# Late modulation chunks in context tile 0, a fixed alternation of expert groups, and output products ahead of the values

## The reference

```python
sh_a, sc_a, gt_a, sh_f, sc_f, gt_f = adaln_params(c, w_mod[l], b_mod[l])
hl = modulate(xl, g_attn[l], sh_a, sc_a)
out_lat, out_ctx = token_mixers(hl, hc, l, not last, w_in[l], ...)
xl = xl + gt_a * out_lat
hl = modulate(xl, g_ffn[l], sh_f, sc_f)
xl = xl + gt_f * expert_choice_ffn(hl, w_router[l], w_gate[l], w_up[l], w_down[l])

def expert_choice_ffn(h, w_router, w_gate, w_up, w_down):
    gates, idx = lax.top_k(affinity, cap)      # cap: 64 latent, 32 context tokens per expert
    a, u = xs @ w_gate, xs @ w_up              # xs: the tokens that each expert chose
    y = (silu(a) * u) @ w_down * gates
```

## Time and profile before

| | us |
|---|---|
| median of three runs | 2147.86 |
| lowest, highest | 2144.3, 2151.32 |
| profiled execution | 2151.53 |
| its span | 2149.7 |
| TensorE busy in the span | 1969.2 (92%) |
| VectorE, ScalarE, GpSimd busy | 664.1, 529.6, 156.6 |
| DMA | 515.66 MB, mean 240 GB/s |
| TensorE's mean granted clock | 0.975 |

### The profile page before, as it was taken

The page is one execution under the profiler, slowest core; times in us unless marked ns, Lnnn a source line. Parts: engine busy times, 40 slices in busy tenths (PEclk is TensorE's granted clock), DMA queues, the critical chain, the costliest instruction groups (busy, mean ns, idle before and its releaser), DMA issues. The chain is left out here.

```text
span 2149.7 us, 27244 instructions
## 1 busy us (share of the span) xinstructions
PE 1969.2 (92%) x10872; PEld 931.5 (43%) x10872; DVE 664.1 (31%) x1746; ACT 529.6 (25%) x1222; POOL 156.6 (7%) x155
## 2 busy tenths in 40 slices
PE   5999989999979999999999899889997998888875
PEld 2436465556642332323323556455554333333322
DVE  3322345666540100101001632366665011110203
ACT  3211154665531000100100421165554110000001
POOL 1101010000010010020100101100001000000000
PEclk9999979999989999999999999999998999999998
DMA  9742020000089999999999402020017899999995
GB/s 353 291 159 81 0 79 1 1 2 1 36 332 414 423 364 418 378 390 421 364 414 421 150 20 79 17 82 1 21 40 286 352 427 426 426 427 427 427 427 217
DMA packets 90935, 515.66 MB, mean 240 GB/s; under 512 B 10594, under 2 KB 15628, under 8 KB 36540
## 3 DMA queue, kind: packets, MB, share of 16 engines
q1 hardware_dynamic: 84496, 493.29, 56.8%
q0 software_dynamic: 4416, 15.21, 2.4%
q10 hardware_dynamic: 1900, 5.43, 0.6%
HBM read 498.69 MB, written 15.20 MB: 239 GB/s over the span
## 5 line engine op out<-in xcount | busy, mean ns | idle before, releaser
L739 PE MATMUL psS<-arena 128*64 128x512 f32 (+9 forms) x4552 | 1158.5, 556 | 71.1 <-DMA arena<-in_w_up 22.0
L739 PEld LDWEIGHTS psS<-arena 128*64 128x64 f32 (+4 forms) x4552 | 456.1, 159 | 666.9 <-issue 585.9
L1961 DVE TENSOR_REDUCE mx<-psS 128x1 f32<-128x768 f32 (+2 forms) x200 | 165.5, 827 | 153.0 <-PE psS L739 151.3
L1307 ACT ACTIVATE arena<-psT 128x768 f32<-128x768 f32 (+7 forms) x261 | 150.1, 577 | 245.7 <-PE psT L742 232.0
L742 PE MATMUL psT<-ident,arena 128*128 128x128 f32 (+1 forms) x1036 | 172.7, 290 | 36.1 <-ACT arena L1307 9.1
L1307 ACT ACTIVATE arena<-psS 128x128 f32<-128x128 f32 (+5 forms) x158 | 61.8, 421 | 571.6 <-PE psS L739 525.7
L2145 DVE TENSOR_TENSOR arena<-arena,psS 128x512 f32<-128x512 f32 x32 | 20.6, 684 | 549.2 <-PE psS L739 549.2
L742 PEld LDWEIGHTS psT<-ident,arena 128*128 128x128 f32 (+1 forms) x1036 | 120.1, 145 | 135.5 <-issue 97.8
L739 PE MATMUL psT<-arena 128*32 128x512 f32 x1536 | 174.5, 595 | 0.0
L1307 ACT ACTIVATE arena<-psS,nb 128x768 f32<-128x768 f32 (+2 forms) x200 | 157.9, 792 | 1.4
L739 PE MATMUL psM<-arena 128*128 128x512 f32 x288 | 140.9, 611 | 0.0
(11 more groups left out here) (226 smaller groups left out, 1266.5 us busy)
## 6 DMA issues: line engine op xcount, KB each, us to landing
arena<-in_w_gate SPq DMA_DIRECT2D x117, 1024.0 KB, 21.3
arena<-in_w_up SPq DMA_DIRECT2D x116, 1024.0 KB, 22.5
arena<-in_w_down SPq DMA_DIRECT2D x116, 1024.0 KB, 25.9
arena<-in_w_mod SPq DMA_DIRECT2D x48, 1024.0 KB, 7.2
arena<-in_w_in SPq DMA_DIRECT2D x6, 2048.0 KB, 7.8
arena<-in_w_out SPq DMA_DIRECT2D x8, 512.0 KB, 7.8
arena<-in_w_out SPq DMA_DIRECT2D x2, 2048.0 KB, 15.4
normed_rows<-arena ACTq DMA_DIRECT2D x8, 512.0 KB, 7.3
```

The costliest lines, as they stand in the source:

```text
L739: return nc.tensor.matmul(o, lhsT, rhs, start=start, stop=stop)
L1307: return nc.scalar.activation(o, i, f, **kw)
L1961: link(V.reduce_max(mx[:, par:par + 1], view(S, 0, P, 0, (512, 2), (1, n)), axis=AX.XY))
```

## The change

The chunks of both late groups are loaded into four places of 1 MB in the region of the output weights (`late_slot`): two once the fourth section is done, the others once the projections are finished, each waiting for the chunk four before. TensorE multiplies them in steps 0 to 11 of context tile 0 (`LATE_AT`), into bank 7 for the first group and bank 5 for the second; ScalarE copies the rows at steps 6 and 12, TensorE turns the groups at steps 16 and 24 (`LATE_TURN_AT`), VectorE copies the columns. The router biases move from steps 3 and 5 to 7 and 8, the gates from 7, 9, 11, 13 to 9, 11, 13, 15. The output weights are loaded behind the chunks, in six transfers. The rings carry expert weights alone. `AHEAD_OF_GATHER` is gone; in the second layer slot 15 waits for the gathered rows.

In the first layer's expert loop every stage has an order of its own: 0, 1, 2 or 2, 0, 1 by `STAGE_ORDER`. Hidden rows are turned in the order 2, 0, 1, and tokens in pairs at four places. Counts and waits follow the orders.

In every attention step of both layers the bias, the gate and the output pieces are issued ahead of the values.

```diff
-AHEAD_OF_GATHER = 6
-GATE_AT = ((7, 9, 11, 13), (9, 11))
-BIAS_AT = ((3, 5), (7,))
+GATE_AT = ((9, 11, 13, 15), (9, 11))
+BIAS_AT = ((7, 8), (7,))
-MOD_LATE, MOD_LAST = KD, KD
-LAST_MOD_AT = {"turn": 13, "columns": 14}
+LATE_AT = {0: (0, 1), 1: (2, 3), 2: (4,), 3: (5,), 4: (6,), 5: (7,), 7: (8, 9), 8: (10, 11), 9: (12,), 10: (13,), 11: (14, 15)}
+LATE_ROW_AT = {6: 0, 12: 1}
+LATE_TURN_AT = {TURNS: 0, TURNS + 8: 1}
+LATE_BANK, LATE_TURN_BANK = (7, 5), 5
+LATE_SLOTS = 4
-TURN_AT = {(8, 1): (0,), (8, 2): (1,), (9, 0): (2,), (9, 1): (3,), (9, 2): (4,), (10, 0): (5,), (10, 1): (6,), (10, 2): (7,)}
+CLL, LLC = (2, 0, 1), (0, 1, 2)
+HIDDEN_AT = {(7, 0): 2, (7, 1): 0, (8, 2): 1}
+STAGE_ORDER = (LLC, CLL, LLC, CLL, LLC, CLL, LLC, CLL, CLL, LLC, CLL, LLC)
+TURN_AT = {(8, 1): (0, 1), (9, 1): (2, 3), (10, 2): (4, 5), (11, 1): (6, 7)}
...
+        def late_slot(c):
+            return WOUT + (4096, 6144, 0, 2048)[c % LATE_SLOTS]
+        def order(l, q, st):
+            if l:
+                return (0, 1)
+            return (2, 0, 1) if q * NSTAGE + st == NQ * NSTAGE - 1 else STAGE_ORDER[st % NSTAGE]
...
+                def late_chunk(c):
+                    _, r, k = MOD_CHUNKS[MOD_FRONT * KD + c]
+                    if c >= LATE_SLOTS:
+                        sp.wait_ge(s_mused, MOD_FRONT * KD + c - LATE_SLOTS + 1)
+                    load(ar[:, late_slot(c):late_slot(c) + SLOT], A["w_mod"][L - 1, k * P:(k + 1) * P, r * 2048:(r + 1) * 2048], s_w[c % 8])
...
+                if l == 0:
+                    sp.wait_ge(z["proj"], NSTEP - TT)
+                    for c in range(2):
+                        late_chunk(c)
                 sp.wait_ge(z["proj"], NSTEP)
...
+                    for c in range(2, 2 * KD):
+                        late_chunk(c)
+                for n, k in enumerate((4, 6, 0, 2)):
+                    if l == 0:
+                        sp.wait_ge(s_mused, (MOD_FRONT + 2) * KD - LATE_SLOTS + n + 1)
...
                     if l and j == NSLOT[l] - 2:
                         sp.wait_ge(z["fgev"], 4 * L)
+                        sp.wait_ge(s_g[1], 16 * L)
-                    if l == 0 and j == FIRST[l] + AHEAD_OF_GATHER:
-                        sp.wait_ge(s_g[2], 16)
...
                         last.then_inc(z["T"], 1)
+                    for c in LATE_AT.get(s, ()) if l == 0 else ():
+                        if c == KD:
+                            pe.wait_ge(z["me"], turns_through(PLANS[l], ("Q", 1, "B1")))
+                        late_mod(c)
+                    if l == 0 and s in LATE_TURN_AT:
+                        g = LATE_TURN_AT[s]
+                        pe.wait_ge(z["me"], turns_through(PLANS[l], ("Q", 2, "B1") if g else ("Q", 1, "C1")))
+                        mod_transpose(MOD_FRONT + g, LATE_TURN_BANK)
+                    if s in BIAS_AT[l]:
+                        router_bias(BIAS_AT[l].index(s))
+                    if s in GATE_AT[l]:
...
+                        gates(2, "gt", (7, 7, 7, 7), (n,))
+                    for x in pieces:
+                        output_piece(*x)
                     if pv is not None:
...
-                    for x in pieces:
-                        output_piece(*x)
                     for x in turns:
...
-                late = range(MOD_FRONT * KD, (MOD_FRONT + 1) * KD) if l == 0 else ()
-                for n in late[:6]:
-                    late_mod(n)
...
-                            for m in last_late[:4]:
-                                late_mod(m)
...
-                    for m in last_late[4:] if l == 0 else ():
-                        late_mod(m)
...
-                        for g in last_order(l) if (q, st) == (NQ - 1, NSTAGE - 1) else range(NX):
-                            if st == 8 and g == 1 and wc:
-                                turn_hidden(q, 2)
+                        for g in (last_order(l) if not wc and (q, st) == (NQ - 1, NSTAGE - 1) else order(l, q, st)):
                             group(q, st, g)
-                            if st == 7 and g == 1:
+                            if wc and (st, g) in HIDDEN_AT:
+                                turn_hidden(q, HIDDEN_AT[st, g])
...
+                    if l == 0 and s in LATE_ROW_AT:
+                        modulation_row(LATE_ROW_AT[s])
...
-                    for g in range(NX):
+                    for g in hidden_order(l):
                         act.wait_ge(z["done"], groups_done(l, q, 3, g))
```

More of the change, by code:

```diff
@@ L430, in backbone_program, with stage_done @@
         s_w = [sem(f"ring_slot{i}") for i in range(max(NSLOT))]
-        MOD_FILLS = [MOD_FRONT if i < KD else 0 for i in range(max(NSLOT))]
+        MOD_FILLS = [L * 3 if i < KD else 0 for i in range(max(NSLOT))]
         NLOAD = NQ * NSTAGE * QUAD
-        FIRST, LAST = (MOD_LATE, 0), (MOD_LAST, 0)
         def slot_filled(l, j):
-            j += FIRST[l]
             i = j % NSLOT[l]
-            earlier = MOD_FILLS[i] + sum(i < NSLOT[k] and (FIRST[k] + NLOAD + LAST[k] - 1 - i) // NSLOT[k] + 1 for k in range(l))
+            earlier = MOD_FILLS[i] + sum(i < NSLOT[k] and (NLOAD - 1 - i) // NSLOT[k] + 1 for k in range(l))
             return s_w[i], 16 * (earlier + j // NSLOT[l] + 1)
-        def late_bank(g):
-            return 7 if g == MOD_FRONT else 3
+        def late_slot(c):
[4 more added lines that the diff above has]
+            return (2, 0, 1) if q * NSTAGE + st == NQ * NSTAGE - 1 else STAGE_ORDER[st % NSTAGE]
         def groups_done(l, q, st, g):
-            return l * NQ * NSTAGE * (SW[0] // P) + (q * NSTAGE + st) * (SW[l] // P) + g + 1
+            return l * NQ * NSTAGE * (SW[0] // P) + (q * NSTAGE + st) * (SW[l] // P) + order(l, q, st).index(g) + 1
+        def stage_done(l, q, st):
+            return groups_done(l, q, st, order(l, q, st)[-1])
         def halves_through(l, i, r):
@@ L979, in _ @@
                         scores(0)
-                    if l and tau == 3:
-                        pe.wait_ge(s_mrow, 3 * L)
-                    if l and tau == LAST_MOD_AT["turn"]:
-                        mod_transpose(MOD_FRONT + 1, 5)
                     for i in k_jobs(tau - 1):
@@ L1210, in turn_hidden @@
                         last.then_inc(z["hp"], 1)
-                        free[6 + b] = (z["he"], 2 * hidden_tile(l, q, g) - 1 + b)
-                last_late = range((MOD_FRONT + 1) * KD, len(MOD_CHUNKS))
+                        free[6 + b] = (z["he"], 2 * hidden_turn(l, q, g) - 1 + b)
                 def combine(q):
@@ L1248, in group @@
                         pe.wait_ge(z["ge"], KD * (q + 1) - 4)
-                    elif q == 0 and m == 0 and g == 0:
+                    elif q == 0 and m == 0 and g == order(l, q, st)[0]:
                         pe.wait_ge(z["ge"], kq + 1)
@@ L1261, in group @@
                         experts, n, col = range(QUAD), CAP_C, 256
-                        for e in experts if (q, st) == (NQ - 1, NSTAGE - 1) else ():
+                        for e in experts if order(l, q, st)[0] == g else ():
                             pe.wait_ge(*slot_filled(l, (q * NSTAGE + st) * QUAD + e))
@@ L1778, in _ @@
                         mod_columns(MOD_T_AT[tau])
-                    if l and tau == LAST_MOD_AT["columns"]:
-                        mod_columns(MOD_FRONT + 1, 5)
                     if tau < NSTEP and uses_dve(*STEPS[tau]):
@@ L2005, in _ @@
                         router_weights()
+                    if l == 0 and s in LATE_TURN_AT:
+                        mod_columns(MOD_FRONT + LATE_TURN_AT[s], LATE_TURN_BANK)
                     for x in summed:
```

123 lines of the change are left out of this document (54 added, 69 removed).

## The result

The changed kernel takes 2166.44 us (median of 4 runs, 2162.38 to 2168.87) against 2148.79 for the kernel before on the same chip: ratio 1.0079, 95% interval 1.0060 to 1.0098. The forecast was 2135.7 with a range of 2126 to 2149; sign and size were wrong. Medians and intervals here are of fast runs; one slow execution of e2 (3338 us) is left out of its interval. The profiled execution of the changed kernel has a span of 2166.8 us, 17.1 above that of before (2149.7).

What follows compares the result with a forecast made beforehand. TensorE was taken to pace the first expert loop with DMA close behind, the weight stream the second. Terms +7 - 2.3 - 3.1 - 3.7 - 0.7 - 5.3 - 0.7 - 3.4 = -12.2 us gave a median of 2135.7, range 2126 to 2149.

Steps and rivals of the forecast that it cites:

- Weights waits: First expert loop: TensorE's waits for weights fall from 4.4 to 1 us, gain 3.4 us (0 to 4.4).
- the rival to which I gave 0.17: First expert loop: weights become the bound and eat the order's and waits' gains, no change, 2145.1 us; chance 0.17.
- My own sign of being wrong: Wrong would be, among others, waits on weights of more than 5 us in the first expert loop.
- Alternation and turns: First expert loop: fewer changes of shape between groups gain 5.3 us, paired token turns 0.7 us.
- Tile 0: Context tile 0, first layer's attention: the moved modulation chunks cost +7 us (3.6 to 17).
- About 22 us: Tile 0, steps 7 to 11: chunks, bias blocks, gates and own work take about 22 us, putting step 12 at 310.
- steps 0 to 5 follow the chunks (to 288): Tile 0: the first six steps are paced by the chunks' arrival, until 288 us.
- Idle time takes in part of the chunks: Tile 0: TensorE's idle 8.8 us, including 1.45 before step 1 and 1.84 ahead of turned outputs, absorbs some chunk work.
- The rival that the clock stays low: Tile 0: TensorE runs at 1.2 GHz between chunk waits; whole tile low gives 2156.7 us, slower; chance 0.10.
- First gather: First layer, ahead of the expert loop: the gather no longer queues behind weights, gain 3.1 us (0 to 3.1).
- second, -3.7 and -0.7 for the projections: Second layer: earlier gather gains 3.7 us (0 to 3.7); a modulation turn leaving the projections gains 0.7 (0 to 1.5).
- End of the first loop: Chunks leave the combine products: first latent product 1.0 us earlier, VectorE's normalised rows then limit; gain 2.3 us together.

Runs made afterwards that it cites:

- e2: Kernel before with only the new expert order (alternating stages, paired token turns, context hidden tile first): 2152.1 us, ratio 1.0023.
- e14: e13 with the new expert order on top: 2137.6 us, ratio 0.9957 to the kernel before.
- e13: Kernel before; gathers for quads 3 and 4 after stage 5, sums' store and load at stage 9, second layer's slot 15 waits for gathers: 2140.2 us, 0.9968.
- e16: Changed kernel, all chunk products but only chunks 0 to 3 loaded, same edit as e6 run again: 2161.7 us, ratio 1.0069.
- e6: Changed kernel with all chunk products, but only chunks 0 to 3 loaded and no wait for the others: 2159.7 us, ratio 1.0042.
- e7: Kernel before with three instead of six weights ahead of the first gather, and second layer's slot 15 waiting for the gathers: ratio 1.0009.
- e4: Changed kernel with the values back ahead of late chunks, router bias, gates and output products in each attention step: ratio 1.0077.

## Why the prediction was wrong, step by step

**Weights waits, forecast -3.4, measured +12.** The step that failed reads "should fall to 1, as 16.8 MB leave a stream of nearly the same length as TensorE's work". The 16.8 MB left at the loop's two ends; the waits stand at stages 3 to 7 of each quad, and nothing had left there. I had divided a total by a total where the trace had five waits, all on in_w_up and so in stages 4 to 7. The next sentence, that a context-first stage needs its last two weights 3.5 us earlier, named the mechanism and priced it at the 1 us left. It was worth about 2.5 us in each quad and 1 more at stage 3 of quads 2 to 4, and it was the rival to which I gave 0.17; and that rival, as I had sized it, stopped at eating the gain. My own sign of being wrong, over 5 us of such waits, came. The DMA share of 0.99 was no measure of slack either: e14's loop is 10 us shorter at a share of 1.00, with 406 GB/s instead of 401.

**Alternation and turns, forecast -6.0, measured -7.5 of TensorE's time** (e13 to e14). Right, a little small. In the changed kernel it is: +12.3 of waits (16.4 of weights and 0.3 for ScalarE, against 4.4), +3.1 for two groups at half clock, -7.5, which makes +7.9 against 8.3 read.

**Tile 0, forecast +7, measured +14.7** (+13.7 between the means of seven profiles each). "About 22 us" for steps 7 to 11 measured 22.15 (296.58 to 318.73), by luck: what I counted there adds up to some 18.6 us (eight chunks at 0.89, bias blocks of 3.43 in all, two gates at 1.02, five times 1.2), and 1.6 of the 22.15 are two chunks at half clock. The failing step is the one before it, "steps 0 to 5 follow the chunks (to 288)": I added the 22 us to 288, as if step 7 began there. Step 6 and the own work of the steps ahead of it were missing, and the low clock from 283 to 290 us lies in them too; step 7 began at 296.58. "Idle time takes in part of the chunks" failed too. Of the idle 8.8 us, 1.45 stand ahead of the first scores and 3.3 behind step 12; 3.7 are left where the chunks went, and there the changed kernel still idles 4.7 (1.09, 3.18 and 0.43). The stall ahead of the turned outputs stayed at 2.16 us where I let it take 1.5 back. The products had to be paid for the most part: 10.6 us of 14.3 even with the clock nearly full (0.96, e16).

**The clock in tile 0.** The rival that the clock stays low did not decide. In 272 to 319 us it was 0.89 after and 0.77 before, and 0.96 in e16. Dips still make the spread between executions (e6 is 5.7 us over e16). Two windows of the changed kernel:

```profile
280.00:285.00 5.00, 1.82 (x10) 0.20 (x9) 0.79 (x4) 1.10 (x4) 0.00 (x0) 0.81 0.96 356
285.00:290.00 5.00, 5.00 (x24) 2.25 (x20) 0.88 (x3) 1.02 (x4) 0.00 (x0) 0.51 1.01 426
```

The dip stands behind the 3.18 us wait, and in 290 to 300 us the clock is at 1.00 again. The later one, at 303.36, has TensorE busy throughout and no wait ahead of it. The Trainium skill, TensorE: Matmul & The Clock Gate, section "HAM oscillation — how this bites in real kernels", says that bursts with DMA waits between them can run at half rate one after another; the trace shows one such stretch here, of some 7 us from 283 to 290 in steps 2 to 4, and not all of steps 1 to 5. The 0.50 in 275 to 280 us of the kernel before, which I counted for the rule, doesn't bear on it: the waits ahead of it were for ScalarE (1.14 and 0.39 us), not for DMA.

**First gather, forecast -3.1, measured -2.4; second, -3.7 and -0.7 for the projections, measured -3.7 together.** The waits in both layers are about what the prediction named (4 us), 3.5 and 4.8 us:

```profile
651.00 1.13 PE L772 MATMUL psS<-ident,arena 128*128 128x128 f32 x4 [3.54 <-DMA arena<-normed_rows,LIU]
...
1687.83 1.13 PE L772 MATMUL psS<-ident,arena 128*128 128x128 f32 x4 [4.83 <-DMA arena<-normed_rows,LIU]
```

e7 adds that in the first layer the gain hangs on a full ring: with three weights held back the gather came 2.2 us sooner and the loop gave back 7.

**End of the first loop, forecast -2.3, measured +1.2** (-0.9 to +1.2 in the experiments with the same tail). The first latent combine product did come 1.0 us nearer, 5.84 us behind the first context product (1207.03) instead of 6.86. But where four chunks had kept TensorE busy it now waits, and goes on at 1.2 GHz:

```profile
1212.87 0.79 PE L769 MATMUL psS<-output_high,selection 128*128 128x512 f32 x1 [3.73 <-DVE output_low L2184]
1213.46 0.63 PE L769 MATMUL psS<-output_low,selection 128*128 128x512 f32 x1
```

Twelve products there start 0.43 us apart and not 0.23: 2.4 us. Behind them TensorE waits 2.27 us for VectorE's rows, as foreseen, and its first eight transposes take 1.97 us instead of the 1.09 of before, at half clock again. I had counted the chunks as work removed and not as what held the clock up.

**Order ahead of the values, forecast 0:** right (e4). **Second expert loop unchanged:** right, 474.98 against 474.85.

## To carry to other kernels

Slack of a stream against an engine is a matter of places, not of totals: list the waits with their times, find what other transfer stands ahead of each, and ask how many buffers are in hand there. An order that needs a buffer sooner spends that slack, and the place of side transfers can be worth more than the order itself: with the new order it was worth 16.2 us of loop (548.8 in e2, 532.6 in e14), the order with the transfers moved 4.3 (e13 to e14). Work that sits where TensorE would otherwise wait, such as the chunks between the combine products, costs little, and here the clock stayed up behind it (1.00, against 0.50 without); moved to where idle time exists only on average, it was paid for the most part.

## What I had not expected of the hardware

Behind a wait of 2.5 us TensorE's next group sometimes took 5.1 to 5.3 us (half clock for part of it) and sometimes 3.64: waits of 2.55 us at 851.61 and 2.58 us at 1150.76 brought no loss, 2.52 us at 988.79 did. And the clock fell to 0.55 in 300 to 310 us of e6, with TensorE busy 10.00 of these 10 us; in e16, the same program, it stayed at 1.00. What decides this stays open.
